# Local attention's softmax scale moved from its probability tiles to its output tiles, a gate loop in two stages, and a new table of steps

## What is computed

```
def mixer_c(hn, pos, w_qkv, b_qkv, sinks, w_o, b_o):      # 16 query heads, 4 key/value heads, 64 wide
    ...
    def block(args):                                       # 128 queries against 256 keys
        sc = jnp.einsum('btkgd,bskd->bkgts', qj, kj) * scale
        sc = jnp.where(valid, sc, -jnp.inf)
        m = jnp.maximum(jnp.max(sc, -1), sink)
        pr = jnp.exp(sc - m[..., None])
        den = jnp.sum(pr, -1) + jnp.exp(sink - m)
        pr = pr / den[..., None]
        return jnp.einsum('bkgts,bskd->btkgd', pr, vj)
    ...
    return o.astype(hn.dtype) @ w_o + b_o
```

## Time and profile before

| | us |
|---|---|
| median of three runs | 3164.46 |
| lowest and highest run | 3161.23, 3169.55 |
| profiled execution, whole time | 3164.53 |
| its span, first to last instruction | 3162.7 |
| TensorE busy in the span | 3104.1 (98%) |
| VectorE, ScalarE, GpSimd busy | 1092.3, 1249.4, 1715.5 |

### The profile page before, as it was taken

The page is one execution under the profiler, slowest core; times in us unless marked ns, Lnnn a source line. Parts: engine busy times, 40 slices in busy tenths (PEclk is TensorE's granted clock), DMA queues, the critical chain, the costliest instruction groups (busy, mean ns, idle before and its releaser), DMA issues. The chain is left out here.

```text
span 3162.7 us, 40836 instructions
## 1 busy us (share of the span) xinstructions
PE 3104.1 (98%) x15422; PEld 2542.0 (80%) x15422; DVE 1092.3 (35%) x2053; ACT 1249.4 (40%) x2262; POOL 1715.5 (54%) x1343
## 2 busy tenths in 40 slices
PE   9999999999999999999999999999999988999999
PEld 7888877788777788788888878878888876788887
DVE  4322321222555423223222674523111349421214
ACT  4332333333544535333222533345333455643334
POOL 5555664565554466465555533247555653565564
PEclk9999999999999999999999999999999999999999
DMA  5333322232222234233333211123333321233332
GB/s 162 101 98 98 96 76 82 84 87 81 71 70 73 68 101 120 80 93 97 98 99 97 74 54 58 48 66 90 97 95 97 100 78 37 78 95 95 100 103 87
DMA packets 149841, 275.26 MB, mean 87 GB/s; under 512 B 16528, under 2 KB 17808, under 8 KB 149520
## 3 DMA queue, kind: packets, MB, share of 16 engines
q1 hardware_dynamic: 149648, 272.66, 29.9%
HBM read 270.50 MB, written 2.10 MB: 86 GB/s over the span
## 5 line engine op out<-in xcount | busy, mean ns | idle before, releaser
L2518 POOL TENSOR_TENSOR WL<-RAW,WH 128x512 fp32r<-128x512 f32 x1002 | 1296.5, 1306 | 872.7 <-ACT WH L2126 871.9
L2126 ACT ACTIVATE WH<-RAW 128x512 fp32r<-128x512 f32 x1002 | 619.2, 627 | 1011.6 <-PE PS L732 952.3
L732 PE MATMUL PS<-HH,WH 128*128 128x512 f32 x2264 | 894.6, 395 | 4.4 <-ACT HH L2126 2.7
L732 PE MATMUL PS<-HL,WH 128*128 128x512 f32 x2264 | 884.1, 391 | 0.9 <-DVE HL L1360 0.9
L732 PE MATMUL PS<-HH,WL 128*128 128x512 f32 x2264 | 884.6, 391 | 0.2 <-POOL WL L2518 0.2
L732 PE MATMUL PS<-AH,WH 128*128 128x512 f32 (+1 forms) x1504 | 583.3, 388 | 4.9 <-ACT WH L2126 2.4
L732 PE MATMUL PS<-AL,WH 128*128 128x512 f32 (+1 forms) x1504 | 580.9, 386 | 3.0 <-DVE AL L1354 2.1
L732 PE MATMUL PS<-AH,WL 128*128 128x512 f32 (+1 forms) x1504 | 580.7, 386 | 0.7 <-POOL WL L2518 0.7
L732 PEld LDWEIGHTS PS<-HH,WH 128*128 128x128 f32 x2264 | 427.0, 189 | 95.1 <-issue 6.3
L732 PEld LDWEIGHTS PS<-HH,WL 128*128 128x128 f32 x2264 | 426.3, 188 | 91.1 <-POOL WL L2518 0.8
L732 PEld LDWEIGHTS PS<-HL,WH 128*128 128x128 f32 x2264 | 426.9, 189 | 87.3 <-DVE HL L1360 2.1
(11 more groups left out here) (231 smaller groups left out, 2449.0 us busy)
## 6 DMA issues: line engine op xcount, KB each, us to landing
RAW<-in_wst SPq DMA_DIRECT2D x1002, 256.0 KB, 2.7
X<-in_x SPq DMA_DIRECT2D x8, 256.0 KB, 5.3
TMP<-in_p SPq DMA_DIRECT2D x8, 256.0 KB, 3.3
out<-X SPq DMA_DIRECT2D x8, 256.0 KB, 2.0
AR<-in_dm SPq DMA_DIRECT2D x1, 1024.0 KB, 7.2
AR<-in_mem SPq DMA_DIRECT2D x1, 1024.0 KB, 5.7
CST<-in_cst SPq DMA_DIRECT2D x1, 612.0 KB, 6.8
AR<-in_pos SPq DMA_DIRECT2D x2, 256.0 KB, 3.0
```

What stands on the lines that cost most here:

```text
L732: return e.matmul(o, l, r, start=a, stop=z, skip_group_check=True)
L2126: return e.activation(o, a, f, **kw)
L2518: return e.tensor_tensor(o, a, b, op)
```

## The change

1. **Scale.** Step sx no longer multiplies the probability tile. VectorE stops at the reciprocal, and GpSimd copies the four reciprocals wide, each over 64 columns, into half of a 128x512 tile (s_rec). Step st waits for the exponentials alone. In step sp, behind the value matmuls, TensorE turns the four 128x128 pieces of s_rec, ScalarE copies the turned tile from PSUM to s_rec, and VectorE multiplies the output tile in PSUM by it. The copy into AH moves from sp to sc.
2. **Gate.** For l = 0, the copy, square and rounding of tile m now stand one step later, behind the sigmoid of tile m+1 (both 6 and 7 in the last step); HL and GpSimd's sums of squares move with them.
3. **Order.** ORDER, its seams and LATE are changed at many places, in all stages behind the first 1000 us.

```diff
+        def behind(k):
+            return ([k - 1] if k else []) + ([7] if k == 7 else [])
...
                 elif kind == "st":
                     n, q = i
-                    e.wait_ge(*at("s_p", n))
+                    e.wait_ge(*at("s_exp", n))
...
                 elif kind == "sp":
                     u = i[0]
                     o, pt = bank("swa_lo", u), s_pt(u)
+                    e.wait_ge(*at("s_turned", 2 * u, 1))
                     e.wait_ge(*at("s_turned", 2 * u + 1, 1))
...
                     z.then_inc(*up("mm", "sp", u))
+                    e.wait_ge(*at("s_rec", 2 * u + 1))
+                    turned(("swa_rb", u), ("swa_rb", u), lambda t: quarter(s_rec(u), t))
...
+        s_rec = lambda u: tmp((0, 1, 4, 6)[u % 4])
...
-                    if l == 0:
-                        e.wait_ge(*at("x_ple", l, m))
-                        low("nc1", m, q, gains(32 + m))
+                    for j in behind(m) if l == 0 else []:
+                        e.wait_ge(*at("x_ple", l, j))
+                        low("nc1", j, psum(*added(l, j)), gains(32 + j))
...
+                    if n > 3:
+                        e.wait_ge(*at("s_rec", n - 4))
                     tt(st[:, 5, :], st[:, 4, :], st[:, 3, :], ADD).then_inc(*up("s_sum", n))
                     e.wait_ge(*at("s_sum", n))
-                    e.reciprocal(st[:, 5, :], st[:, 5, :]).then_inc(*up("s_rec", n))
-                    e.wait_ge(*at("s_rec", n))
-                    tt(s_p(n), s_p(n), st[:, 5, :].unsqueeze(2).to_broadcast([128, 4, 256]), MUL).then_inc(*up("s_p", n))
+                    e.reciprocal(st[:, 5, :], st[:, 5, :]).then_inc(*up("s_inv", n))
+                elif kind == "sp":
+                    u = i[0]
+                    e.wait_ge(*at("swa_rb", u))
+                    tt(psum("swa_lo", u), psum("swa_lo", u), s_rec(u), MUL).then_inc(*up("swa_scaled", u))
...
-                    if l == 0:
-                        e.wait_ge(*at("x_ple", l, m))
-                        if m == 6:
+                    for j in behind(m) if l == 0 else []:
+                        e.wait_ge(*at("x_ple", l, j))
+                        if j == 6:
                             e.wait_ge(*at("mm", "pf", 0, 7))
-                        act(x(m), q, ACT.Copy).then_inc(*up("x_kept", "nc1", m))
-                        square("nc1", m, q)
-                        high("nc1", m, q, gains(32 + m))
+                        q = psum(*added(l, j))
+                        act(x(j), q, ACT.Copy).then_inc(*up("x_kept", "nc1", j))
+                        square("nc1", j, q)
+                        high("nc1", j, q, gains(32 + j))
...
                 elif kind == "sp":
                     u = i[0]
-                    e.wait_ge(*at("mm", "sp", u))
+                    e.wait_ge(*at("mm", "swa_rb", u))
+                    act(s_rec(u), psum("swa_rb", u), ACT.Copy).then_inc(*up("swa_rb", u))
+                elif kind == "sc":
+                    u = i[0]
+                    e.wait_ge(*at("swa_scaled", u))
                     act(AH[:, u, :], psum("swa_lo", u), ACT.Copy).then_inc(*up("swa_hi", u))
...
+                elif kind == "sx":
+                    n = i[0]
+                    st = small("f", ("s_st", n % 4), 24).rearrange("p (a c) -> p a c", a=6)
+                    e.wait_ge(*at("s_inv", n))
+                    if n > 7:
+                        e.wait_ge(*at("swa_scaled", n // 2 - 4))
+                    e.tensor_copy(half(s_rec(n // 2), n % 2), st[:, 5, :].unsqueeze(2).to_broadcast([128, 4, 64])).then_inc(*up("s_rec", n))
```

Of the table, two lines near the seam of the feed-forward and one of LATE show the kind of edit:

```diff
-        ("grow", "nab", 0), ("pf", 0, 2), ("pf", 0, 3), ("grow", "nab", 1), ("hp", "nf0", 0), ("grow", "nab", 2), ("hp", "nf0", 1), ("u_open", 0, 0),
+        ("grow", "nab", 0), ("pf", 0, 2), ("hp", "nf0", 0), ("pf", 0, 3), ("grow", "nab", 1), ("grow", "nab", 2), ("hp", "nf0", 1), ("u_open", 0, 0),
...
+        ("sc", 3): 4, ("sp", 4): 4, ("sc", 4): 4, ("sv", 2): 2, ("sv", 3): 2, ("sv", 4): 2, ("sv", 5): 2, ("sv", 6): 2, ("sv", 7): 2,
```

More of the change, by code:

```diff
@@ L435 @@
         ("d_sm", 7, 0), ("mq", 0), ("d_sm", 7, 1), ("d_turn", 7, 0), ("d_sc", 7, 2), ("mq", 1), ("d_sc", 7, 3), ("d_turn", 7, 1), ("d_sm", 7, 2),
-        ("d_t2", 6), ("mq", 2), ("d_turn", 7, 2), ("d_turn", 7, 3), ("d_sm", 7, 3), ("mq", 3),
+        ("d_t2", 6), ("mq", 2), ("d_turn", 7, 2), ("d_sm", 7, 3), ("d_turn", 7, 3), ("mq", 3),
     ],
@@ L454 @@
         ("fac", "na"), ("ab_open", 6), ("ab_open", 7), ("ab_gl",), ("bc", "na"), ("ab_gt",), ("gv", 0), ("c", 0, 1), ("m_v", 0, 0), ("c", 0, 0),
-        ("m_v", 0, 3), ("m_v", 0, 4), ("m_v", 0, 5), ("m_v", 0, 1), ("c", 0, 2), ("m_v", 0, 2), ("gv", 1), ("m_v", 0, 6), ("fq", 0), ("fk", 0),
[4 rows of a table removed]
+        ("m_v", 0, 3), ("m_v", 0, 4), ("m_v", 0, 5), ("m_v", 0, 1), ("c", 0, 2), ("fk", 0), ("m_v", 0, 2), ("gv", 1), ("m_v", 0, 6), ("fq", 0),
[4 rows of a table added]
         ("m_tri", 0, 3), ("m_sc", 0, 3), ("xs", 2), ("l", 1, 2, 0), ("l", 1, 1, 2), ("m_n", 0), ("m_d", 0), ("l", 1, 2, 1), ("l", 0, 2, 1),
@@ L473 @@
         ("m_tri", 2, 2), ("l", 3, 1, 2), ("m_sc", 2, 1), ("l", 2, 2, 0), ("m_sc", 2, 2), ("l", 2, 2, 1), ("l", 3, 2, 0), ("l", 2, 2, 2),
[5 rows of a table removed]
-        ("m_sc", 3, 2), ("m_tri", 3, 3), ("s", 3, 1, 0), ("s", 2, 1, 1), ("m_sc", 3, 3), ("s", 3, 1, 1), ("s", 2, 2, 0), ("m_n", 3), ("m_d", 3),
[5 rows of a table added]
+        ("m_sc", 3, 2), ("s", 3, 0, 1), ("m_tri", 3, 3), ("s", 3, 1, 0), ("m_sc", 3, 3), ("s", 3, 1, 1), ("s", 2, 2, 0), ("m_n", 3), ("m_d", 3),
         ("s", 3, 2, 0), ("s", 2, 2, 1), ("m_f", 3), ("o_open", "w_out_ab_2", 0), ("s", 2, 3, 0), ("s", 3, 2, 1), ("m_fin", 3), ("s", 2, 3, 1),
@@ L490 @@
     [
+        ("pf", 0, 4), ("fac", "ns0"),
+    ],
+    [
         ("so", 0), ("e", 0, 6), ("e", 0, 7), ("so", 1), ("so", 2), ("so", 3), ("so", 4), ("so", 5), ("so", 6), ("fac", "nc1"), ("so", 7), ("sv", 0),
[12 rows of a table removed]
[12 rows of a table added]
         ("to", "nco", 1), ("to", "nco", 2), ("to", "nco", 3), ("to", "nco", 4), ("to", "nco", 5), ("to", "nco", 6), ("to", "nco", 7), ("fac", "nco"),
-        ("pf", 1, 1), ("bc", "nco"), ("grow", "nco", 0), ("pf", 1, 2), ("pf", 1, 3), ("grow", "nco", 1), ("hp", "nf1", 0), ("grow", "nco", 2),
+        ("pf", 1, 1), ("bc", "nco"), ("grow", "nco", 0), ("pf", 1, 2), ("pf", 1, 3), ("hp", "nf1", 0), ("grow", "nco", 1), ("grow", "nco", 2),
         ("hp", "nf1", 1), ("u_open", 1, 0), ("grow", "nco", 3), ("hp", "nf1", 2), ("u_open", 1, 1), ("grow", "nco", 4), ("hp", "nf1", 3),
@@ L508 @@
         ("grow", "nco", 7), ("hp", "nf1", 6), ("u_open", 1, 5), ("hp", "nf1", 7), ("u_open", 1, 6),
+    ],
+    [
+        ("pf", 1, 4), ("fac", "ns1"),
     ]
@@ L515 @@
         + ORDER[1]
-        + between(("mg", 2, 1), ("wo", 7))
+        + between(("mo", 2), ("wo", 7))
         + ORDER[2]
@@ L519 @@
         + ORDER[3]
-        + between(("u_open", 0, 7), ("e", 0, 6))
+        + between(("u_open", 0, 7), ("fac", "ns0"))
         + ORDER[4]
-        + between(("u_open", 1, 7), None))
+        + between(("pf", 0, 5), ("e", 0, 6))
+        + ORDER[5]
+        + between(("u_open", 1, 7), ("fac", "ns1"))
+        + ORDER[6]
+        + between(("pf", 1, 5), None))
 LATE = {
@@ L530 @@
         ("d_sm", 2, 3): -2, ("d_sm", 3, 3): -2, ("d_sm", 5, 3): -2, ("d_sm", 6, 3): -2, ("d_sm", 7, 3): -2, ("g", 0, 0): 2, ("g", 1, 0): 2,
[4 rows of a table removed]
[5 rows of a table added]
+        ("m_tri", 0, 2): -1, ("grow", "nab", 1): -3, ("fq", 0): 4,
     },
@@ L2620, in gpsimd @@
                     gather(("ns0", "ns1")[i[0]], i[2])
-                elif kind == "e" and i[0] == 0 and 0 < i[1] <= last("nc1"):
-                    gather("nc1", i[1])
+                elif kind == "e" and i[0] == 0:
+                    for j in behind(i[1]):
+                        if j:
+                            gather("nc1", j)
                 elif kind == "sr":
```

## The result

The changed kernel takes 3128.97 us (median of four runs, 3127.33 to 3131.85) against 3163.82 of the kernel before in the same comparison. The ratio is 0.9887, with a 95% interval of 0.9873 to 0.9900. The gain is 34.9 us where 21.0 were forecast, and the time lies 1.0 us under the range. The profiled execution took 3128.1 us, its span is 3126.3, 36.4 less than before.

A forecast was written before the change was run, and what follows sets the result against it. TensorE, busy 3104.1 of 3162.7 us, was taken as the bound, with VectorE fuller only in the local attention. Terms -8.1 - 6.5 - 2.7 - 2.7 - 1.0 = -21.0 us from 3164.5 gave 3143.5 us, range 3130 to 3157.

The forecast's parts named there:

- local attention: Local attention stage: removed waits and two slow stretches, less added turns and new waits, give -8.1 us, bounds -18.8 and +3.
- gate: Gate loop in two stages: earlier panel casts end 3.1 us of waits and 3.4 us of clock loss, -6.5 us.
- seams, and fac at its new place: Feed-forward seams: HH ahead of the evacuation shortens TensorE's waits, -2.7 us; fac behind pf 4 counted as nothing.
- two single waits: TensorE's waits at d_turn 7 3 (1.66 us) and mo 3 (1.01 us) go by reordering, -2.7 us.
- delta rule: Delta-rule stage: some 25 steps move by one to four places, -1 us, bounds -8 and +8.
- The turns' -8.7: Local attention: six waits of turns for VectorE's reciprocal product, 8.7 us in all, lose their cause.
- The rope entry: Local attention's start: 1.8 of the 2.2 us wait for the first rotated query tile goes.
- The bound passes from VectorE to TensorE: Local attention: VectorE falls to 83.7 us of work, against TensorE's least of 91.2 us.
- TensorE closes up: Rival: local attention at -15 and delta rule at -4 give 3133.6 us; chance 0.18.
- GpSimd is the bound: Rival: GpSimd's copy delays panel casts and rotation products; 4 us of wait per unit gives 3175.5 us; chance 0.04.
- The new chain takes the place of the old wait: Rival: local attention's 8 units each cost 1 us more than allowed, its gain goes, 3151.6 us; chance 0.20.
- The price weighed by a page: Local attention: GpSimd's 16 copies might each hold VectorE up 0.76 us, forecast 3 us later; not used in the sum.

The follow-up runs named there:

- fourfold copies: Changed kernel with each of GpSimd's 16 wide reciprocal copies made four times in a row; 3132.4 us.
- load kept: Changed kernel with 16 unused maxima over a 128x1024 constant added on VectorE, about the load the change took out; 3138.41 us.
- planted wait: Changed kernel with 7 TensorE waits added in each layer's feed-forward, in two runs with different wait lengths; 3164.03 and 3185.01 us.

## Why the prediction was wrong

The direction, VectorE's sum and most of the mechanisms were right; four of five terms were too small. Of the 15.4 us between the forecast's -21.0 and the span's -36.4, 11.0 lie in TensorE's busy time (-15.0 where -4.0 was forecast: the clock) and 4.4 in its idle time (-21.4 where -17.0 was).

| term | forecast | by the traces | run alone |
|---|---|---|---|
| local attention | -8.1 | -15.1 | -13.0 |
| gate | -6.5 | -6.5 | -7.3 |
| seams, and fac at its new place | -2.7 | -6.1 | -10.8 with the next |
| two single waits | -2.7 | -4.6 | |
| delta rule | -1.0 | -4.7 | -7.9 |

The column by the traces adds to -37.0; the first 1000 us took 0.5 more, and rounding is the rest to -36.4.

**The clock was mis-sized, and this is the main failure.** The sum took 3.4 us for it in the local attention, 3.4 at the gate, nothing elsewhere. In the records 37.5 us of half clock went, worth up to 18.8. By stage: local attention four stretches of four, 6.8 us instead of 3.4; gate 3.4 as forecast; delta rule 20.5 us of half clock down to 10.2; one stretch each at the d_turn wait and in both parts with a seam, 1.7 us a piece, against one new one at 1183. The d_turn wait of 1.66 us was costed at its row; the stretch of 3.4 us right behind it was visible and was put only into the bound. Counting half of the stretches in the local attention was wrong too, and so was the reading "each behind such a wait". Two stand right behind a turn's wait, of 2.34 and 2.12 us; the other two right behind waits of 1.25 us for AL and 1.64 for ACC, each about 2 to 4 us behind a turn's wait of 1.45 and 1.69. All of these turn's waits were to go. The sixteen traces tell what belongs to the change and what to the single execution:

| place | traces with a slow stretch, old form | new form |
|---|---|---|
| gate loop | 7 of 7 | 0 of 9 |
| local attention (scale and order both old, or both new) | 6 of 6, 6.8 to 13.7 us | 0 of 6 |
| d_turn 7 3 | 4 of 5 | 0 of 11, but 7 have the one at 1183 |
| seam of layer 0 | 4 of 5 | 0 of 11 |
| norm sums ahead of the seam of layer 1 | 2 of 5 | 4 of 11 |
| delta rule, all half clock | 20.5 to 27.3 us, mean 23.9 | 6.8 to 20.5 us, mean 13.0 |

So the 1.7 us at layer 1's seam are luck of the two profiled executions: that stretch (2747.5 to 2750.9) stood ahead of the seam's wait (from 2753.4), behind one of 0.65 us for the norm sums, which both kernels have. At the other places most traces of the old form have a stretch and those of the new one have none, or in the delta rule about half as much; but what goes at d_turn comes back at 1183 in 7 of 11.

Not all of it is the change's steady gain. The runs of one kernel differ by their mean granted clock and by little else: 16 of the kernel before's runs at 0.993 average 3161.1 us, 10 at 0.990 average 3169.8. Three at 0.996 average 3155.6, where the changed kernel's one at 0.996 took 3131.8. By that one run the gain at equal clock is, as an estimate, about 24 us, and the clock gives the other 11; that is less than 18.8, and part of a slow stretch often lies in a wait.

**Local attention, the waits.** The turns' -8.7 was right to the digit (8.74 to none). The rope entry gave 1.3 of 1.8: 2.17 us became 0.83. The failed step is "I allow 2.0 us more for new waits inside", with 1.0 at the tail: the other waits, 3.8 us before, were 3.1 after, so -0.7 where +3.0 was put. The tail wait is 0.22, and old waits on banks went as new ones came. The turns' +2.8 agrees: TensorE's busy time fell by 4.2 us, that is 6.8 of clock less 2.8. So -8.7 - 1.3 - 0.7 - 6.8 + 2.8 = -14.7, against 15.1 measured.

**"The bound passes from VectorE to TensorE" was half of the reason.** It is true of the final kernel, but the scale alone made VectorE lighter by about as much (18.9 us) and gave 3 us, ratio interval up to 1.0001. The forecast read the waits' end off the removal; it takes the new step order, and that order without the removal is no better than the old one, by stage and medians worse (166.1 against 161.3 us). The prediction costed the new chain and not the old order's fit to it. One of its signs of being wrong came, VectorE's idle time on ScalarE's copies (10.9 us), and meant nothing for TensorE here; another, the delta rule by over 5 us, came in the run alone (7.9) and not between the two traces (4.7).

**Seams.** The wait changed its releaser instead of going: 1.36 to 0.99 and 1.35 to 1.41 us, plus the two waits of 0.29 on HL that did go, 0.9 us of the 2.7 forecast. The failed step is "the new order puts HH ahead": the evacuation was next, and in layer 1 it was held back by HH. These parts gained all the same, by two slow stretches (3.4, of which layer 1's 1.7 are luck) and fac (some 0.8 in waits of 0.2 that went); about 1 us of the 6.1 is not placed.

**Two single waits** both went, -2.7, plus 1.7 of clock. **The gate** was right at -6.5, and so was its cover of the casts. **The delta rule** lost 1.6 us of waits by the rows, near the 1 us; the rest is clock, and its size changes from run to run: profiled executions with this same new table (changed kernel, fourfold copies, load kept) show 10.2, 13.7 and 20.5 us of half clock there, the old table 20.5 or more in all five.

**The rivals.** "TensorE closes up" (3133.6) was nearest: -15 for the local attention and -4 for the delta rule, as between the traces; it lacked the single stretches elsewhere. Its reason, 7.5 us of spare time on VectorE, was not enough: with the scale alone VectorE had that room and the stage stayed. "GpSimd is the bound" is refuted by the fourfold copies. "The new chain takes the place of the old wait" is what the waits look like with the old order.

**The price weighed by a page.** With 48 more copies on GpSimd, VectorE's busy time in the stage was 90.9 us against 91.8: no VectorE time was lost to the copies. The rule of the Trainium skill, page "GPSIMD Engine Reference", section "Key points", is that the two engines contend when VectorE has two SBUF inputs. The traces agree, but for other instructions: the small sums that stay, 128x4 with two SBUF inputs, last about 0.15 us, and 4 of the 16 in the changed kernel last 0.83 to 1.25, each beside a GpSimd subtraction and until its end:

```profile
2668.40 1.25 DVE L1373 TENSOR_TENSOR SM<-SM 128x4 f32<-128x4 f32 x1
```

```profile
2668.35 1.28 POOL L2546 TENSOR_TENSOR WL<-RAW,WH 128x512 fp32r<-128x512 f32 x1 [2.58 <-ACT WH L2149]
```

Such sums cost 5.9 us in the stage before and 6.2 now. Most of VectorE's wide instructions left in it read PSUM for one input, so the copies could meet little that the rule names; the 0.76 us for each of 16 copies did not come.

## What to carry to other kernels

When waits of about 2 us or more on TensorE go, count the slow stretch behind each as part of the wait: 1.6 us each here, and so nearly doubling its price; waits under 1.5 us, alone in dense work, cost themselves and 0.3 us. Between two traces, credit a slow stretch to an edit only if other traces of the same form agree; one stretch here came and went with the same steps and the same wait around it. Taking a step out of a chain is worth what the step order lets through: run removal and order as a square of four, since each alone can be worth nothing. When a seam's order is changed so that one of two results comes first, look at which the engine then waits for, and whether the early one waits itself and holds the other.

## What the runs showed of the hardware

- A planted wait of 1.45 us never cost TensorE its full clock in 7 cases (layer 0) and one of 2.11 did in 5 of 7 (layer 1); of equal waits some lose it and some not, and waits of 3.45 us gave half-clock stretches of 3.4 and 6.8 us in turn. Slow stretches also stood behind sums of squares, matmuls of one column: around a wait of 0.65 us between two rows of eight in 6 of 16 traces, and behind 16 of them without a wait in 7 of 11.
- Between executions slow stretches come and go, and waits away from them stay: the first five of the local attention (2.17, 2.34, 2.12, 1.45, 1.25 us) are the same to 0.02 us in the kernel before and the runs of the delta rule and of the seams alone, which have the same four stretches; where two stretches are missing (the gate alone), 2.12 became 2.46 and waits of 0.65 and 0.84 came. Nearly the whole spread of the kernel before, 3155 to 3174 us over 66 runs, goes with the mean granted clock, 0.988 to 0.996.
- GpSimd's copy of 128x4 numbers spread to 128x256 takes 0.40 us, between its memset of 0.31 and its product of 0.76.
- A VectorE sum of 128x4 with two SBUF inputs, 0.15 us by itself, lasted 1.25 us beside a GpSimd subtraction of 128x512 and ended with it.
